# Delta rule heads: the inverse is applied once per chunk to a difference, with two dense blocks per chunk

## The reference, cut to what matters

```python
Lmat = where(strict, (kb @ k.T) * decay, 0)          # kb = k * beta
sol  = triangular_solve(eye + Lmat, [v * beta, kb * exp(gc)])
value, k_cumdecay = sol[..., :DV], sol[..., DV:]
def step(state, xs):
    v_new = val - kcd @ state
    o     = qd @ state + a_c @ v_new
    state = state * gl + kd.T @ v_new
```

## Time and profile before

| | us |
|---|---|
| median of 3 runs (1929.74 to 1930.17) | 1929.79 |
| the profiled execution, its time | 1931.19 |
| the profiled execution, its span | 1929.2 |
| PE busy | 1882.4 |
| VectorE busy | 1194.5 |
| ScalarE busy | 792.7 |
| GpSimd busy | 298.4 |

### The profile page before, as it was taken

The page is one execution under the profiler, slowest core; times in us unless marked ns, Lnnn a source line. Parts: engine busy times, 40 slices in busy tenths (PEclk is TensorE's granted clock), DMA queues, the critical chain, the costliest instruction groups (busy, mean ns, idle before and its releaser), DMA issues.

```text
span 1929.2 us, 29736 instructions
## 1 busy us (share of the span) xinstructions
PE 1882.4 (98%) x10628; PEld 1528.4 (79%) x10628; DVE 1194.5 (62%) x1844; ACT 792.7 (41%) x1495; POOL 298.4 (15%) x222
## 2 busy tenths in 40 slices
PE   7999999999999899999999999999999999999997
PEld 6888878888887677777778888888787888888885
DVE  5997554333333767777745856737679568476474
ACT  4234443233233555555533423424456534243242
POOL 2532222111012200000101100101212211011012
PEclk9999989999999899999999999999999999999998
DMA  5233323232322111111112332232221223323231
GB/s 195 93 105 98 131 66 109 88 100 97 98 92 94 44 54 64 61 61 53 59 45 87 110 109 87 87 109 88 100 87 56 64 89 102 107 85 100 88 109 66
DMA packets 46945, 170.47 MB, mean 88 GB/s; under 512 B 5344, under 2 KB 5504, under 8 KB 46720
## 3 DMA queue, kind: packets, MB, share of 16 engines
q1 hardware_dynamic: 45648, 165.12, 25.8%
q10 hardware_dynamic: 1200, 3.95, 0.6%
HBM read 166.94 MB, written 2.11 MB: 88 GB/s over the span
## 4 chain that ended last, share of the span: by engine, by line
PE 92%; DVE 4%; ACT 2%; issue 1%; DMA 0%; POOL 0%; DVEq 0%; POOLq 0%; SPq 0%
PE ps L275 19%; PE ps L277 18%; PE ps L276 18%; PE ps L263 9%; PE ps L264 9%; PE ps L265 9%; PE ps L651 1%; PE ps L676 1%; PE ps L696 1%; PE ps L314 1%; PE ps L315 1%; DVE scr L1533 1%; PE ps L320 1%; DVE scr L1524 1%; DVE Y L1524 1%
## 5 line engine op out<-in xcount | busy, mean ns | idle before, releaser
L227 DVE TENSOR_TENSOR w_lo<-w_raw,w_hi 128x1024 fp32r<-128x1024 f32 x255 | 345.3, 1357 | 144.4 <-ACT w_hi L222 143.7
L222 ACT ACTIVATE w_hi<-w_raw 128x1024 fp32r<-128x1024 f32 x304 | 316.9, 1050 | 273.1 <-PE ps L277 175.1
L275 PE MATMUL ps<-A_hi,w_hi 128*128 128x512 f32 x896 | 368.3, 411 | 13.4 <-DVE w_lo L227 10.4
L277 PE MATMUL ps<-A_hi,w_lo 128*128 128x512 f32 x896 | 351.0, 392 | 0.0
L276 PE MATMUL ps<-A_lo,w_hi 128*128 128x512 f32 x896 | 350.4, 391 | 0.0
L275 PE MATMUL ps<-B_hi,w_hi 128*128 128x512 f32 x688 | 271.9, 395 | 2.9 <-issue 1.8
L277 PE MATMUL ps<-B_hi,w_lo 128*128 128x512 f32 x688 | 268.1, 390 | 0.0
L276 PE MATMUL ps<-B_lo,w_hi 128*128 128x512 f32 x688 | 267.9, 389 | 0.0
L275 PEld LDWEIGHTS ps<-A_hi,w_hi 128*128 128x128 f32 x896 | 169.0, 189 | 50.7 <-issue 14.2
L277 PEld LDWEIGHTS ps<-A_hi,w_lo 128*128 128x128 f32 x896 | 168.8, 188 | 36.6
L276 PEld LDWEIGHTS ps<-A_lo,w_hi 128*128 128x128 f32 x896 | 169.3, 189 | 28.6
(11 more groups left out here) (294 smaller groups left out, 2531.2 us busy)
## 6 DMA issues: line engine op xcount, KB each, us to landing
w_raw<-d_ws SPq DMA_DIRECT2D x304, 512.0 KB, 3.5
X<-d_xT SPq DMA_DIRECT2D x4, 512.0 KB, 7.8
X<-d_xT ACTq DMA_DIRECT2D x1, 2048.0 KB, 8.1
d_out<-X SPq DMA_DIRECT2D x4, 512.0 KB, 2.6
scr<-gc_rows ACTq DMA_DIRECT2D x7, 256.0 KB, 3.1
cst<-d_cst SPq DMA_DIRECT2D x1, 800.0 KB, 11.5
par<-d_par SPq DMA_DIRECT2D x1, 344.5 KB, 3.0
scr<-d_pw SPq DMA_DIRECT2D x1, 256.0 KB, 12.1
```

Of the source, the lines that this page charges most:

```text
L222: nc.scalar.activation(w_hi[:, c], raw[:, c], ACT.Copy).then_inc(S(f"w_hi{s}"), 1)
L227: nc.vector.tensor_tensor(w_lo[:, c], raw[:, c], w_hi[:, c].bitcast(F32), ALU.subtract)\
L275: pe.matmul(ps[bank][:], w_hi[:, c], hi, start=k == 0, stop=False)
L277: last = pe.matmul(ps[bank][:], w_lo[:, c], hi, start=False, stop=k == total - 1)
```

## The change

The solve is applied to a difference. Before: VN = inverse * VR - (inverse * KG) * state. After: VN = inverse * (VR - exp(gc) * (K * state)), so KG and WT are not made. On PE, for chunks 1 to 3, keys times state goes to bank 5, VectorE forms exp(gc) * that - VR in place of VR (a new semaphore `d_sub`), PE multiplies by the inverse, and VectorE copies with factor -1 to VN. The product within a chunk is issued one chunk later. Each chunk has two dense blocks (`between`), one behind the inverse product and one behind the KD product; the blocks behind the loop are fewer by as many. The first products of a head (gram) go to banks 3 and 2 instead of 4 and 3, and the wait for the squares of k and q (`d_sq`) moves from in front of them to in front of the first transposes of the inverse. On VectorE the convolution op of a chunk moves from behind the new state to in front of it.

```diff
@@ delta_pe
-            pe.wait_ge(S("d_sq"), at("d_sq", 2 * NCH))
             for c in range(NCH):
-                last = pe.matmul(ps[4 - c // 2][:, (c % 2) * 256:(c % 2 + 1) * 256], KQv[:, c, 0, :],
+                last = pe.matmul(ps[3 - c // 2][:, (c % 2) * 256:(c % 2 + 1) * 256], KQv[:, c, 0, :],
                                  KQ[:, c * 256:(c + 1) * 256], start=True, stop=True)
...
             pe.wait_ge(S("zeros"), count("zeros", ZEROS))
+            pe.wait_ge(S("d_sq"), at("d_sq", 2 * NCH))
...
-            for i in range(2):
-                pe.wait_ge(S("d_tt"), at("d_tt", 13 + i))
-                if i == 0:
-                    pe.matmul(chunk(ps[3], 0), tt_of(0), chunk(VR, 0), start=True, stop=True).then_inc(S("d_pv"), 1)
-                for c in (2 * i, 2 * i + 1):
-                    last = pe.matmul(chunk(ps[4 + i], c % 2), chunk(KG, c), tt_of(c), start=True, stop=True)
-                last.then_inc(S("d_pw"), 1)
+            def between(n):
+
+                if more:
+                    part((18 + n) // KT, (18 + n) % KT, 1)
+                else:
+                    out_part(2, n, n + 1)
             for c in range(NCH):
-                val = ps[3 + 4 * (c % 2)][:, 0:P]
+                if c % 2 == 0:
+                    pe.wait_ge(S("d_tt"), at("d_tt", 13 + c // 2))
                 if c:
-                    pe.wait_ge(S("d_wt"), at("d_wt", c // 2 + 1))
                     pe.wait_ge(S("d_s"), at("d_s", c))
-                    pe.matmul(val, chunk(WT, c), ST[c % 2], start=False, stop=True).then_inc(S("d_pv"), 1)
+                    pe.matmul(ps[5][:, 0:P], KQv[:, c, 0, :], ST[c % 2], start=True, stop=True).then_inc(S("d_ks"), 1)
+                    pe.matmul(chunk(ps[6], c - 1), LAv[:, c - 1, 1, :], VN[(c - 1) % 2], start=c == 1, stop=True)
                     pe.matmul(chunk(ps[6], c), chunk(QD, c), ST[c % 2], start=True, stop=False)
-                if c < NCH - 1:
-                    pe.matmul(ps[3 + 4 * ((c + 1) % 2)][:, 0:P], tt_of(c + 1), chunk(VR, c + 1), start=True, stop=False)
+                    pe.wait_ge(S("d_sub"), at("d_sub", c))
+                pe.matmul(ps[3 + 4 * (c % 2)][:, 0:P], tt_of(c), chunk(VR, c), start=True, stop=True)\
+                    .then_inc(S("d_pv"), 1)
+                between(2 * c)
                 pe.wait_ge(S("d_vn"), at("d_vn", c + 1))
                 if c < NCH - 1:
                     pe.matmul(ps[2][:, (c % 2 + 1) * P:(c % 2 + 2) * P], chunk(KD, c), VN[c % 2],
                               start=True, stop=True).then_inc(S("d_ps"), 1)
-                if more:
-                    part(2, 2 + c, 1)
-                elif c:
-                    if c == 1:
-                        pe.wait_ge(S("d_wt"), at("d_wt", 2))
-                    out_part(2, 2 * (c - 1), 2 * c)
-                last = pe.matmul(chunk(ps[6], c), LAv[:, c, 1, :], VN[c % 2], start=c == 0, stop=True)
-            last.then_inc(S("d_po"), 1)
+                    between(2 * c + 1)
+            pe.matmul(chunk(ps[6], NCH - 1), LAv[:, NCH - 1, 1, :], VN[(NCH - 1) % 2], start=False, stop=True)\
+                .then_inc(S("d_po"), 1)
             if more:
-                part(2, 6, 2)
+                part(3, 1, 1)
                 token_major_kq(pe, head_count(h + 1))
-                part(3, 0, 4)
+                part(3, 2, 3)
...
             if more:
-                part(3, 4, 4)
+                part(3, 5, 3)
@@ delta_act
-            act.wait_ge(S("d_ro"), at("d_ro", 0))
-            token_scale(act, "d_kvr", KG, 5, lambda c: head_col(EGC, h, c))
...
-            for i in range(2):
-                act.wait_ge(S("d_pw"), at("d_pw", i + 1))
-                a.activation(WT[:, 2 * i * P:2 * (i + 1) * P], ps[4 + i][:, 0:2 * P], ACT.Copy, scale=-1.0)\
-                    .then_inc(S("d_wt"), 1)
@@ delta_dve
             for c in range(NCH):
+                val = ps[3 + 4 * (c % 2)][:, 0:P]
+                if c:
+                    dve.wait_ge(S("d_ks"), at("d_ks", c))
+                    v.scalar_tensor_tensor(out=chunk(VR, c), in0=ps[5][:, 0:P], scalar=head_col(EGC, h, c),
+                                           in1=chunk(VR, c), op0=ALU.mult, op1=ALU.subtract).then_inc(S("d_sub"), 1)
                 dve.wait_ge(S("d_pv"), at("d_pv", c + 1))
-                v.tensor_copy(VN[c % 2], ps[3 + 4 * (c % 2)][:, 0:P]).then_inc(S("d_vn"), 1)
+                if c:
+                    v.tensor_scalar(VN[c % 2], val, -1.0, None, ALU.mult).then_inc(S("d_vn"), 1)
+                else:
+                    v.tensor_copy(VN[0], val).then_inc(S("d_vn"), 1)
+                if c == 0:
+                    conv(1, 1)
+                elif c == 1:
+                    dve.wait_ge(S("d_la"), at("d_la", 5))
+                    conv(0, 4)
+                elif c == 2:
+                    conv(1, 2)
+                else:
+                    conv(1, 3)
                 if c < NCH - 1:
                     dve.wait_ge(S("d_ps"), at("d_ps", c + 1))
...
-                if c == 0:
-                    conv(1, 1)
-                elif c == 1:
-                    dve.wait_ge(S("d_la"), at("d_la", 5))
-                    conv(0, 4)
-                elif c == 2:
-                    conv(1, 2)
-                else:
-                    conv(1, 3)
```

More of the change, by code:

```diff
@@ L517, in build @@
         LAv = LA.rearrange("p (c n t) -> p c n t", c=NCH, n=2)
-        XB, WT = carve_y(T), carve_y(T)
+        XB = carve_y(T)
         TC, TTC, TTF = carve_y(NCH * 64), carve_y(NCH * 64), carve_y(T)
@@ L549, in build @@
         PER = dict(d_c0=3, d_tap=9, d_th=4, d_qkv=3, d_gate=1, d_sq=8, d_tr=2, d_trv=1, d_gb=16,
-                   d_gram=2, d_s1=4, d_sq_eps=1, d_sqk=1, d_mask=1, d_dt=4, d_eg=1, d_la=5, d_kvr=12, d_tt=14, d_t=2, d_ptr=2,
-                   d_px=12, d_x=16, d_pt=12, d_ttr=10, d_ttc=12, d_pw=2, d_wt=2, d_pv=4, d_vn=4,
+                   d_gram=2, d_s1=4, d_sq_eps=1, d_sqk=1, d_mask=1, d_dt=4, d_eg=1, d_la=5, d_kvr=8, d_tt=14, d_t=2, d_ptr=2,
+                   d_px=12, d_x=16, d_pt=12, d_ttr=10, d_ttc=12, d_pv=4, d_ks=3, d_sub=3, d_vn=4,
                    d_po=1, d_ps=3, d_s=3, d_osq=4, d_oms=1, d_orow=1, d_o1=4, d_ro=1, d_o2=1, o_hi=1, o_lo=1)
@@ L708, in delta_pe @@
                         if i:
-                            pe.wait_ge(S("d_kvr"), at("d_kvr", 2 * NCH))
+                            pe.wait_ge(S("d_kvr"), at("d_kvr", NCH))
                     else:
@@ L730, in delta_pe @@
                         if i:
-                            pe.wait_ge(S("d_kvr"), at("d_kvr", 3 * NCH))
+                            pe.wait_ge(S("d_kvr"), at("d_kvr", 2 * NCH))
                         pe.wait_ge(S("d_o1"), at("d_o1", 0))
@@ L764, in delta_pe @@
                               start=True, stop=True).then_inc(S("d_ps"), 1)
-                if more:
-                    part(2, 2 + c, 1)
-                elif c:
-                    if c == 1:
-                        pe.wait_ge(S("d_wt"), at("d_wt", 2))
-                    out_part(2, 2 * (c - 1), 2 * c)
-                last = pe.matmul(chunk(ps[6], c), LAv[:, c, 1, :], VN[c % 2], start=c == 0, stop=True)
-            last.then_inc(S("d_po"), 1)
+                    between(2 * c + 1)
+            pe.matmul(chunk(ps[6], NCH - 1), LAv[:, NCH - 1, 1, :], VN[(NCH - 1) % 2], start=False, stop=True)\
+                .then_inc(S("d_po"), 1)
             if more:
-                part(2, 6, 2)
+                part(3, 1, 1)
                 token_major_kq(pe, head_count(h + 1))
-                part(3, 0, 4)
+                part(3, 2, 3)
             else:
-                out_part(2, 6, KT - 1)
                 out_part(3, 0, 5)
@@ L897, in delta_act @@
             act.wait_ge(S("d_orow"), at("d_orow", 1))
+            act.wait_ge(S("d_ro"), at("d_ro", 0))
             token_scale(act, "d_o1", KG, 6, lambda c: TK[:, 28 + c:29 + c])
@@ L961, in delta_dve @@
                 dve.wait_ge(S("d_dt"), at("d_dt", c + 1))
-                g = ps[4 - c // 2][:, (c % 2) * 256:(c % 2 + 1) * 256].rearrange("p (n t) -> p n t", n=2)
+                g = ps[3 - c // 2][:, (c % 2) * 256:(c % 2 + 1) * 256].rearrange("p (n t) -> p n t", n=2)
                 v.scalar_tensor_tensor(out=LAv[:, c, :, :], in0=g, scalar=TK[:, 16 + c:17 + c],
```

## The result

| | us |
|---|---|
| before, median of 6 (1929.32 to 1930.27) | 1929.76 |
| after, median of 6 (1936.80 to 1939.23) | 1938.32 |
| after / before, 95% interval | 1.0043 (1.0031 to 1.0055) |
| the profiled execution after, time and span | 1938.76, 1937.0 |

The account below looks back on a forecast made before the run. PE, busy 98%, was taken as the bound, with two chains behind VN(3) becoming late: +10.5 - 1.3 - 1.0 = +8.2, shaded to +7.7 us, 1937.5. The range was 1932.0 to 1941.5.

Parts of the forecast that it names:

- seven heads: Looped heads of the delta stage: next gram at 18.03 against 16.53, +1.5 us per head, +10.5 for seven.
- first head: Gram no longer waits for the squares, but the first inverse seed is not earlier: -1.3 us, bounds 0 to -1.7.
- last head: No next head's convolutions, fixed scalars; chunk 3 ends earlier and the gain passes through: -1.0 us, bounds -0.6 to -1.2.
- rival A: Behind VN(3), late convolution and split/evacuation chains make PE wait 1.0 and 0.7 before two transposes; +6 to +10 us, chance 0.50.
- The price of the looped scalar: VectorE's subtraction: a head-indexed scalar adds 0.11 us when VectorE arrives idle.
- B: Tight chunk loop: no 0.11 for the register, state in time; +3.7 us, about 1933.5, chance 0.20.
- C: Work behind VN(3) not really late, only L750 and old waits count; -5 us, 1924.7, chance 0.06.
- D: Spill: VectorE's lateness at the gram reaches the inverse's first transposes, 0.3 more per head; +10 us, 1940, chance 0.17.
- E: Each looped head's waits of 1.0 and 0.7 lower PE's clock; +14 us, above 1945, chance 0.07.
- The rule against small ops: Skill's fixed cost gives 0.26 us per VectorE op from PSUM, the sum 1.9 less; the prediction kept the rows' longer times.

Follow-up runs that it names:

- e4: Kernel before with only the gram products in banks 3 and 2 and the wait for the squares behind them; 1928.48 against 1929.24 us, ratio 0.9994.
- e1: Changed kernel with only VectorE's order altered: next head's convolution taps and splits moved from behind VN(3) into idle time behind each new state; 1927.87 us, 0.9991 of before.
- e2: Changed kernel with four more small products (KD by inverse, read by nobody) on PE just in front of transposes L616; 1937.59 us, 1.0041 of before.
- e3: Changed kernel with the subtraction's scalar from a fixed column instead of one addressed by head number; 1934.82 us, 1.0030 of before.
- e8: e1 with both decay scalars copied by ScalarE into fixed columns at the head's start; 1924.73 us, 0.9975 of before.
- e9: e8 with dense work cut into single matmuls, seven per chunk, ten before the output transposes; 1923.14 us, 0.9965 of before.
- e6: Changed kernel with VectorE's convolution op moved back behind the new state; 1937.65 us, 1.0044 of before.
- e5: Changed kernel with the dense blocks of the seven looped heads back where they stood before, one per chunk; 1941.05 us, 1.0059 of before.
- e7: e1 with the looped heads' dense blocks cut into single matmuls, spread over the chain's gaps; 1926.15 us, 0.9986 of before.
- e10: e8 with the spread of e7, six single matmuls per chunk, nine before the output transposes; 1923.65 us, 0.9970 of before.
- e11: Changed kernel with five small products, read by nobody, in PE's last head alone; 1937.44 us, 1.0040 of before.

## Why the prediction was right, step by step

| step | predicted | measured |
|---|---|---|
| subtraction ready after K times state | 0.95 | 0.94 |
| inverse products of chunks 1 to 3 | 2.79, 5.82, 8.85 | 2.77, 5.83, 8.83 |
| VN(3) on VectorE | 9.38 | 9.36 |
| L616 | 11.79 | 11.77 |
| output transposes | 15.42 | 15.30 |
| next gram | 18.03 | 17.87 |
| seven heads | +10.5 | +9.4 |
| first head | -1.3 | -1.7 |
| last head | -1.0 | +0.7 |
| ahead of the stage | 0 | -0.45 |

The seven heads: from the first L760 of the first head to that of the last, 696.54 to 992.64 is 296.10, against 698.72 to 985.42, 286.70, before: +9.4, or 1.34 a head. The first head: L616 to the first inverse product is 29.13 against 30.86. PE then waits 1.3 for VectorE's seed, as the prediction said; the gain is larger because PE had been late for that seed in the profiled execution before, at half clock: the seed was ready on VectorE at 675.81, and PE came to it at 677.66. e4 has the same 29.14 from this edit alone. The stage itself was reached 0.45 earlier (L616 at 667.41 against 667.86) through the same instructions as before; over all the traces that time lies between 666.00 and 667.86. With it the sum is 9.4 - 1.7 + 0.7 - 0.45 = 8.0; the spans differ by 7.8.

The total agrees better than its parts. The seven heads were 1.1 too high, the first head 0.4 and the approach 0.45; the last head was 1.7 too low, through a fall of the clock that the prediction had not put there, and that cancelled most of the other misses. Without that fall the spans would differ by some 6.2 instead of 7.8 (an estimate). The medians differ by 8.6 and the two profiled executions by 7.6, as the one before lay 1.4 above its median. That 1937.5 came within 0.8 is in part luck; the mechanism and the times within a head are not.

**Two late chains behind VN(3)** (rival A): shown by e1 for both and by e2 for the first. The first wait was 1.0 in starts, the second 0.6, where 0.7 was predicted.
**The price of the looped scalar**, 0.11: shown by e3 and e8. It is paid also when VectorE is busy until just before (e1), so I had its condition wrong: in chunks 2 and 3 of e1 it is 0.61 and 0.63 from K times state to the subtraction, in e8, with fixed columns, 0.49 and 0.44. That the register instruction begins only when the wait has ended would fit, but no run separates it.
**B** fell with it. **C** fell: L616 stands right behind L916. Its floor is near e1, which is the changed kernel with those chains short: equal to before per head (286.73 and 286.70 for the seven).
**D** did not occur in the changed kernel: the first-level products of the inverse (L597) do not wait in the looped heads. It came in e9, where PE is quicker.
**E**, the clock, did not act in the looped heads: the granted clock stays 1.00 there, with 1.2 us of waits in each head. It did act in the last head of the profiled execution, and there the term -1.0 failed. Windows of the kernel after in the last head (columns as in the earlier trace rows):
```profile
991.00:992.00 1.00, 0.45 (x12) 0.32 (x6) 0.43 (x2) 0.93 (x4) 0.00 (x0) 1.00 0.00 0
...
993.00:994.00 1.00, 1.00 (x5) 0.81 (x5) 0.32 (x2) 0.00 (x0) 0.00 (x0) 0.50 0.00 0
...
995.00:996.00 1.00, 1.00 (x4) 0.81 (x3) 0.29 (x1) 0.00 (x0) 0.00 (x0) 0.50 0.00 0
```
The first inverse product to the first block behind B_lo is 18.10 there. In e1 and e3, at full clock, it is 16.54, and before it was 17.40: the structure gave -0.9, close to the forecast, and the clock cost 1.6. The Trainium skill, "TensorE: Matmul & The Clock Gate", section "What's actually happening", lets the gate follow how busy PE has been; by that, the trace agrees here (PE was busy 0.45 of the us ahead). The trace before shows no fall behind the same waits: PE was busy 0.41 of the us from 984 to 985, and the clock stayed at 1.00. The fall does not need the changed chunk loop. In the last head it stands in the traces of the changed kernel, e2, e6 and e9, and also of e4, which has the chunk loop of before; it is absent before and in e1, e3, e5, e7, e8 and e10, where the same three waits (0.33, 0.55, 0.18) stand, and in e11, which filled the last two. Each is one execution, and executions of one kernel differ in their clock: the 26 of the kernel before on the chip of e4 have a mean clock of 0.989 in five (1930.77 to 1931.22) and of 0.991 in 21 (1928.18 to 1930.39). So the traces cannot tell whether a program has this fall or an execution has it. What decides it is open, and so is how much of 1.6 is in the medians.

**The rule against small ops.** The subtraction took 0.35, not the 0.26 of the Trainium skill's "VectorE: DVE Perf Modes", section on the TRN2 errata (an estimate from that page). The measurement decides; the VN op with its factor took 0.29 like the copy.

## What to carry to other kernels

When an engine is busy 98% of the time, removing its work helps only if what it reaches next is ready earlier too. List the waits that are just covered, with their spare time; filler (independent work) moved from behind a dependency to in front of it is taken from that spare. Then look at the other engine's order: here the filler of VectorE had to move with that of PE. That alone took the loss away (e1, whose seven heads are equal to before), and with fixed scalars and single matmuls as filler the change became a small gain (e8 0.25%, e9 0.35%).

Do not read a term of 1 or 2 us off a single pair of profiled executions: compare the same stretch in several traces first. The approach to the stage, with the same instructions, differed by 1.9 from trace to trace, and the last head by 1.6 through the clock.

## What was new about the hardware

- A scalar operand whose address is computed from a loop register delayed a VectorE op by 0.10 to 0.11 behind a wait. In the traces three such ops a head are 2.2 us over seven heads (e3), five a head 3.5 (e8 against e1).
- A small matmul that comes out of a wait gives its result up to 0.1 later than one in a stream (in e3, with a fixed scalar, 0.50 and 0.53 against 0.43 from its start), and the next small product starts 0.30 after it instead of 0.22. In e7 this took back 0.10 of the 0.15 by which the KD product came sooner.
- The granted clock can fall to 1.2 GHz for some 3 to 4 us behind short waits (0.33, 0.55 and 0.18 within 2 us), which cost 1.4 to 1.6 us. The same three waits stand in the last head of 12 of the 13 traces (e11 filled the last two), and the clock fell behind them in 5.
